# Adding the four channel tiles on GpSimd ahead of the mean matmul, and a bias copy issued from ScalarE

## What is computed

```python
h = rmsnorm(x, pre_norm_g[l])
u = h @ w_in[l]
q, k, v, g_att, c_val, c_glu, g_conv = jnp.split(u, split_pts, axis=-1)
a = chunk_attention(q, k, v, rel_bias[l]) * jax.nn.silu(g_att)
c = conformer_conv(c_val, c_glu, dw_w[l], dw_b[l], conv_ln_g[l], conv_ln_b[l],
                   w_pw[l], b_pw[l]) * jax.nn.silu(g_conv)
y = jnp.concatenate([a, c], axis=-1) @ w_out[l]
x = x + rmsnorm(y, post_norm_g[l])
```

## Time and profile before

| | us |
|---|---|
| median of 3 runs | 2664.9 |
| lowest and highest run | 2659.37, 2668.94 |
| span of the profiled execution | 2665.6 |
| PE busy | 2384.7 |
| DVE busy | 1711.2 |
| ACT busy | 962.0 |
| POOL busy | 292.4 |

### The profile page before, as it was taken

One profiled execution on the slowest core, in us unless ns is written; L12 is line 12 of the kernel. 1 busy time (PEld: TensorE's weight loads), 2 busy tenths in 40 slices (PEclk: granted clock), 3 DMA queues, 4 the chain that ended last, 5 costly groups with the idle time before them and its releaser, 6 DMA issues. The chain is left out here.

```text
span 2665.6 us, 45368 instructions
## 1 busy us (share of the span) xinstructions
PE 2384.7 (89%) x16468; PEld 2197.2 (82%) x16468; DVE 1711.2 (64%) x3174; ACT 962.0 (36%) x1803; POOL 292.4 (11%) x260
## 2 busy tenths in 40 slices
PE   5999999999997899999997889993898888889887
PEld 5999999999996889888986667782787778878886
DVE  5756656656557887888886534432666766676675
ACT  4111111111113221222121534432666666666664
POOL 0000000000000000000000000000322332232242
PEclk9999999999998999999998899995999999999998
DMA  5222222222224433332333342327466456646743
GB/s 176 100 96 73 92 87 75 95 82 86 99 71 153 163 115 138 135 128 105 131 123 112 105 119 90 126 75 207 113 172 160 119 151 163 162 120 177 179 119 119
DMA packets 207901, 327.46 MB, mean 123 GB/s; under 512 B 16625, under 2 KB 141561, under 8 KB 207768
## 3 DMA queue, kind: packets, MB, share of 16 engines
q1 hardware_dynamic: 206680, 324.69, 40.3%
q10 hardware_dynamic: 1088, 1.05, 0.2%
HBM read 198.24 MB, written 127.46 MB: 122 GB/s over the span
## 5 line engine op out<-in xcount | busy, mean ns | idle before, releaser
L261 PE MATMUL p_pb<-h_hT_hi,p_w_hi 128*128 128x256 f32 x3072 | 873.8, 284 | 39.4 <-DVE h_hT_lo L204 24.6
L263 PE MATMUL p_pb<-h_hT_hi,p_w_lo 128*128 128x256 f32 x3072 | 864.5, 281 | 0.0
L262 PE MATMUL p_pb<-h_hT_lo,p_w_hi 128*128 128x256 f32 x3072 | 864.4, 281 | 0.0
L261 PEld LDWEIGHTS p_pb<-h_hT_hi,p_w_hi 128*128 128x128 f32 x3072 | 581.7, 189 | 45.4 <-DVE p_st L455 22.6
L262 PEld LDWEIGHTS p_pb<-h_hT_lo,p_w_hi 128*128 128x128 f32 x3072 | 582.4, 190 | 0.7
L263 PEld LDWEIGHTS p_pb<-h_hT_hi,p_w_lo 128*128 128x128 f32 x3072 | 581.7, 189 | 0.0
L638 DVE SCALAR_TENSOR_TENSOR p_acc<-p_hgl,k_dwt,p_acc 128x512 f32<-128x512 f32 x544 | 368.3, 745 | 0.0
L423 DVE SCALAR_TENSOR_TENSOR p_acc<-p_hg,k_dwt,p_acc 128x256 f32<-128x256 f32 x832 | 337.3, 478 | 0.0
L1349 DVE CUSTOM_DVE_ANT_0 p_pr<-p_s,p_bias 128x640 f32<-128x640 f32 (+4 forms) x256 | 199.8, 781 | 207.0 <-PE p_s L1451 205.5
L1266 ACT ACTIVATE p_pr<-p_pr,p_nmax 128x640 f32<-128x640 f32 (+4 forms) x256 | 204.0, 797 | 189.2 <-DVE p_nmax L1349 187.1
L1451 PE MATMUL p_s<-p_ks,p_q_hi 128*128 128x384 f32 (+2 forms) x480 | 178.5, 376 | 103.0 <-DMA p_q_lo<-q_parts 61.7
(11 more groups left out here) (155 smaller groups left out, 3891.4 us busy)
## 6 DMA issues: line engine op xcount, KB each, us to landing
h_x<-in_x SPq DMA_DIRECT2D x32, 1024.0 KB, 6.3
q_parts<-p_st SPq DMA_DIRECT2D x64, 256.0 KB, 2.3
k_parts<-p_st SPq DMA_DIRECT2D x64, 256.0 KB, 2.4
v_parts<-p_vst SPq DMA_DIRECT2D x16, 1024.0 KB, 4.4
y_conv<-p_yst SPq DMA_DIRECT2D x64, 256.0 KB, 2.0
p_ks<-k_parts SPq DMA_DIRECT2D x32, 512.0 KB, 8.8
p_vs<-v_parts SPq DMA_DIRECT2D x16, 1024.0 KB, 11.5
p_y<-y_conv SPq DMA_DIRECT2D x16, 1024.0 KB, 6.3
```

The costliest lines, as they stand in the source:

```text
L261: nc.tensor.matmul(out, stat_hi(k), mov_hi(k), start=(k == 0), stop=False)
L262: nc.tensor.matmul(out, stat_hi(k), mov_lo(k), start=False, stop=False)
L263: mm = nc.tensor.matmul(out, stat_lo(k), mov_hi(k), start=False, stop=(k == tiles - 1))
```

## The change

POOL gets two additions per block: `pairs` (channel tiles 0 and 1 plus 2 and 3, 128x1024) and `total` (the two halves of `pairs`, 128x512). `mean` on PE becomes one matmul with `total`. PE now waits for `total_ok` where it waited for `acc_in`. POOL waits for `acc_in`, and before it overwrites `total` for `mean_ps` of the block before. The copy of `rev` moves from SP's stream (behind block 0's stores) to ACT's (behind block 0's copies of output units), with its wait for `rev_ok`; SP's block 0 goes into the loop.

```diff
+            def channels(i, first=False):
+                pool.wait_ge(acc_in, DMA * (i + 1))
+                nc.gpsimd.tensor_tensor(pairs[:, :, :], acc[:, 0:2, :], acc[:, 2:4, :], ALU.add).then_inc(pairs_ok, 1)
+                pool.wait_ge(pairs_ok, i + 1)
+                if not first:
+                    pool.wait_ge(mean_ps, i)
+                nc.gpsimd.tensor_tensor(total[:, :], pairs[:, 0, :], pairs[:, 1, :], ALU.add).then_inc(total_ok, 1)
...
-            body(0, 2)
-            sp.wait_ge(rev_ok, 2)
-            sp.dma_start(D["rev"], rev[:, None, :].broadcast_to([HEADS, P, 3 * P - 1])).then_inc(rev_out, DMA)
-            with sp.Fori(1, NBLK - 2) as i:
+            with sp.Fori(0, NBLK - 2) as i:
...
             body(0, False)
+            act.wait_ge(rev_ok, 2)
+            act.dma_start(D["rev"], rev[:, None, :].broadcast_to([HEADS, P, 3 * P - 1])).then_inc(rev_out, DMA)
             with act.Fori(1, NBLK - 1) as i:
...
             def mean(i, first=False):
-                pe.wait_ge(acc_in, DMA * (i + 1))
+                pe.wait_ge(total_ok, i + 1)
                 if not first:
                     pe.wait_ge(dev_ok, i)
-                for c in range(CT):
-                    mm = nc.tensor.matmul(mean_b[:, :], K["ones"][:, :], acc[:, c, :], start=(c == 0), stop=(c == CT - 1))
-                mm.then_inc(mean_ps, 1)
+                nc.tensor.matmul(mean_b[:, :], K["ones"][:, :], total[:, :], start=True, stop=True).then_inc(mean_ps, 1)
```

More of the change, by code:

```diff
@@ L730, in pass_3 @@
         sqs = T.sb("sqs", [P, 2, BLK])
+        pairs, total = T.sb("pairs", [P, 2, BLK]), T.sb("total", [P, BLK])
+        pairs_ok, total_ok = T.sem("pairs_ok"), T.sem("total_ok")
         var_s, rstd = T.sb("var", [P, 4]), T.sb("rstd", [P, 4])
@@ L789, in norm @@
                 nc.gpsimd.tensor_tensor(rstd[:, :], var_s[:, :], K["mhalf"][:, :], ALU.pow).then_inc(rstd_ok, 1)
-            with pool.Fori(0, NBLK) as i:
+            def channels(i, first=False):
[5 more added lines that the diff above has]
+                nc.gpsimd.tensor_tensor(total[:, :], pairs[:, 0, :], pairs[:, 1, :], ALU.add).then_inc(total_ok, 1)
+            channels(0, True)
+            norm(0)
+            with pool.Fori(1, NBLK) as i:
+                channels(i)
                 norm(i)
```

## The result

| | us |
|---|---|
| kernel before, median of 18 runs | 2668.35 (2659.37 to 2677.01) |
| changed kernel, median of 18 runs | 2656.43 (2650.78 to 2668.10) |
| ratio | 0.9962, 95% interval 0.9948 to 0.9975 |
| changed kernel, profiled execution | 2667.74, span 2666.0 |

By the ratio the change gains 0.38% (0.25 to 0.52), 10 us, where 25 were forecast; the two medians lie 11.9 us apart. The time lies outside the range of 2633 to 2655. In this comparison the kernel before took 3.4 us more than in the three runs that the forecast was set against; 0.9962 of those 2664.9 us is 2654.8, just inside the end of the range. That doesn't mend the forecast: less than half of the gain is there.

What follows compares the result with a forecast made beforehand. PE's own work and one stall in one block were taken to set pass 3's length. From 2665.6 us, 15.5 (mean) and 9.4 (copy) gave a span of 2640.7, a median of 2640 us; range 2633 to 2655.

Steps and rivals of the forecast that it cites:

- The mean on PE: Pass 3, blocks 2 to 7: six matmul records fewer save 2.6 us a block, 15.5 us in all.
- rival 1: Block 1 of pass 3: the stall stays, only the mean's gain is left, 12.9 to 16.5 us; chance 0.26.
- The additions on POOL: Pass 3 blocks: additions take 3.7 us, `total` is ready 10 us before PE asks for it; cost 0.
- The first two means: Start of pass 3, where PE isn't full: 0, with ends of 0.5 us won or 1.5 us lost.
- The copy of `rev`: Block 1 of pass 3: moving the copy to ACT's queue shortens PE's stall; gain 9.4 us.
- The first count: Stalled block: packets alternate, copy keeps its pace, PE stalls 2.8 us instead of 10.2; gain 9.4 us, chance 0.45.
- The second count: Stalled block: packets alternate and their times add up, PE stalls 9.1 us and drops its clock; gain 1 us.
- ACT and SP: Block 0 of pass 3: the copy's 1.20 us issue fits before ACT's square, cost 0; freed SP time gains 0.
- Rival 4: Block 0 of pass 3: ACT is held by the copy's issue, PE runs dry; 3.8 us slower, 2669; chance 0.03.

Runs made afterwards that it cites:

- second pair: The kernel before and the changed kernel, both unchanged, one more profiled execution each on one chip: 2664.9 and 2660.0 us.
- adds_only: The changed kernel with the copy of `rev` back in SP's stream: 2662.4 us beside 2672.7 for the kernel before, ratio 0.9961.
- copy_only: The kernel before with only the copy of `rev` moved to ACT: 2670.0 us, ratio 0.9990 (0.9971 to 1.0009).
- sixteen_timed: The changed kernel with `rev` on 16 partitions instead of 8, 64 repetitions from each: 2644.2 us beside 2667.6 for the kernel before, ratio 0.9910.
- wide: The changed kernel with `rev` on 128 partitions instead of 8, each written 8 times: 2649.9 us beside 2672.7 for the kernel before, ratio 0.9913.
- wide_sp: The kernel wide with its copy issued by SP, not ACT: 2644.3 us beside 2669.7 for the kernel before, ratio 0.9902.
- split: The changed kernel with the 8-partition copy issued from SP in eight pieces, one behind each block's stores: 2642.6 and 2646.8 us, ratios 0.9901 and 0.9923.

## Why the prediction was wrong

**The mean on PE: right.** 2.6 us a block was forecast. An ordinary block from `gc` to `gc` went from (241.1 - 50.7) / 5 = 38.1 us to (224.8 - 47.3) / 5 = 35.5. The timeline of PE, to be held against the earlier trace rows:

```profile
1577.58 1.02 PE L958 MATMUL p_mean<-p_total,k_ones 128*128 128x512 f32 x2
1578.03 0.79 PE L261 MATMUL p_pw<-p_s_hi,p_pw_hi 128*128 128x512 f32 x1
1578.66 0.39 PE L262 MATMUL p_pw<-p_s_lo,p_pw_hi 128*128 128x512 f32 x1
```

From the mean's start to the product's successor are 1.08 us; less 0.23 it is 0.43 for each of two records. But only five of the six blocks keep the saving. The sixth is the stalled one, where it is swallowed, as rival 1 had it.

**The additions on POOL: right on time, incomplete on cost.** POOL's timeline in a steady block:

```profile
1598.79 2.40 POOL L792 TENSOR_TENSOR p_pairs<-p_acc 128x1024 f32<-128x1024 f32 x1 [5.85 <-DMA p_acc<-conv]
1601.27 1.63 POOL L796 TENSOR_TENSOR p_total<-p_pairs 128x512 f32<-128x512 f32 x1
```

`total` is there at 1602.9, where 1603.5 was forecast; the next mean comes one block (35.5 us) after 1577.58, at 1613.1, so the cover is 10 us. No PE time is lost in any steady block. What the working didn't ask is what POOL's work does to DVE: 15.8 us more of busy time over 8 blocks, 2 us a block. DVE has room for that beside PE, everywhere but at the start.

**The first two means: a failed step, small.** Forecast 0, with ends of 0.5 us won and 1.5 us lost. The start takes 2.1 us longer (51.86 for 49.73; 2.3 in the second pair), beyond the lower end. The working asked when the mean is done. It was done about as worked out (2.04 us from 1487.17, which is 33.4 us after the pass's start; forecast 1485.4 - 1452.5 = 32.9). Two things came behind that. One it didn't have: DVE runs three two-input subtractions beside the additions. The other it named for the lower end and priced too low: PE, with less to do, gets its full clock about 10 us later. The first product comes 2.0 us later in the first pair and 0.5 in the second; how the loss divides between the two wasn't measured. The Trainium skill, page "SBUF — State Buffer", section "SBUF: two separate sides", says that VectorE with two inputs from SBUF and GpSimd share one pair of ports, and that one of them holds it for a whole instruction while the other is blocked. These rows agree in direction: DVE's three went from 3.49 to 6.00 us, and POOL's 128x512 took 2.12 us where pass 4 has 1.29; POOL's 128x1024 was not slower (2.35 us for 2.38).

**The copy of `rev`: the failed step that decides.** The first count took it that the copy's and SP's packets alternate on the shared engines from the issue of `gc` on, while the copy keeps its pace, so that `gc` and the first store are through at 1557.3, 19.5 us after the issue of `gc`. From that follow a stall of 2.8 us on PE and a gain of 9.4 us. What the runs showed in its place: for 14.3 us after its issue the shared half of `gc` isn't served at all, then the queues alternate, and the copy doesn't keep its pace (28 rows a us for 32). `gc` lands 23.2 us after its issue, `acc` 25.2 (25.6 before), the stall is 9.8 us, and the clock is at 0.50 behind it. In the sum, the gain of 9.4 us by the stall came out as 0.8: the stalled block costs 47.28 - 35.54 = 11.7 us more than an ordinary one, where before it cost 12.6 (11.8 in the second pair, and the gain there is nothing). By adds_only the 3.4 us by which that block is shorter divide otherwise: nothing for its mean, about 3 for the copy.

The second count (stall of 9.1 us, gain 1) came out nearly to the number, but by luck. It lets the packets alternate from the start at 0.34 us a pair. In the trace a pair takes 8 / 28 = 0.29 us on each of eight engines, and the time is lost ahead of the alternation, which no count had. Why it begins so late stays open.

Two things were wrong in choosing. The share of 1.13 from pass 4 was of transfers from and to 128 partitions, and was carried over to engines which one slow transfer keeps for 0.43 of the possible 0.50. And the row that said more was read for the queue alone: `acc`'s issue held for 4.42 us. It is held for 4.43 us when the copy isn't on SP's queue, so the copy's place in that queue can't have been the only reason.

The prediction leaned on the Trainium skill, page "DMA: Bandwidth & Descriptors", section "Queues, rings and completion order", for an alternation packet by packet. The section speaks of packets of several descriptors; the count took one row of 1.5 KB or 2 KB as a packet. The trace has both: 14 us without a switch, which doesn't fit row by row, and then 84 packets beside 84. The prediction's other rule, from the Trainium skill, page "DMA: Bandwidth & Descriptors", section "Issuing engines are not separate DMA queues", is that another issuer saves only the sequencer's time. The 15.5 us put down for it are nearer to the 10 us measured, and to the 13 to 14 us in pass 3, than the forecast's 24.9. The trace agrees with it but for some 2 us: counted from the issue of the copy, `gc` landed after 35.9 us, in adds_only after 37.6.

**ACT and SP: right.** The issue takes ACT 1.33 us, and the square still waits 2.65 us for DVE behind it, as forecast (2.7). Rival 4 didn't happen.

**Where the sum ends.** 15.5 + 9.4 - 0 = 24.9 became, in pass 3, 16.3 - 2.1 = 14.2 us (13.2 in the second pair): five means of 2.6, the stalled block shorter by 3.4 us, and 2.1 lost in the start. Rival 1 (the stall stays), with 12.9 to 16.5 us, is what happened in pass 3. The whole kernel shows 10 us, with an interval of 7 to 14. That pass 4 gave 3 us back is possible (868 to 874 us for 863 to 864.5) but two executions of each can't show it.

## What to carry to other kernels

In these runs the pace of a copy went with its source pattern, and a second queue took other transfers past it only late (after 14 us, and then row for row): read the share and the GB/s of the stretch in which it runs alone before you count on another queue, and widen the transfer over more partitions, or cut it so that it ends before the next one is due (here 12 us, where moving it brought about 3). Before shortening the work between two fixed events, ask what sets the later one: PE's saving in the block with the stall was swallowed because the stores came when the copy let them. And moving work from TensorE to GpSimd had a second price on VectorE, and went with a later full clock where TensorE had little to do; look for the place where VectorE is on the path or the clock has yet to rise, not at the blocks with room.

## What the runs showed of the hardware

- An SBUF-to-DRAM copy of 1532 KB in rows of 1532 bytes depends on the number of source partitions: from 8 it ran at 48 GB/s with a share of 0.43 (some 32 us, an estimate from its size and that rate), from 16 at 97 GB/s with 0.87 (landed after 18.8 us), from 128 it landed after 9.1 us. From 8 to 16 the share doubles, from 16 to 128 each engine gets faster. That a partition read over and over is the limit fits, but the repetitions, the number of partitions and the part of the 128 over which they spread changed together, and none was varied alone. The same 8 rows spread over all 128 partitions, for one, weren't tried.
- Beside a slow copy on ACT's queue, the part of SP's transfers on the same engines waited for 14.3 us after the issue (changed kernel), while the copy kept its 32 rows a us; then the two queues moved 84 packets each in 3 us, and the copy 28 rows a us. copy_only shows the same.
- SP's issue of `acc`, 0.41 us in other blocks, was held for 4.43 and 4.38 us with the slow copy on ACT's queue (after, copy_only), and for 4.42 and 5.53 us with it on SP's own (before, adds_only).
- In the start of pass 3 TensorE's granted clock first rose from 0.50 to 1.00 at 29 to 33 us after it had 5.3 to 6.0 us of matmuls in the second mean or while it ran them, and at 41 to 44 us where the second mean was 2.0 us with a gap of 2.1 us behind it (five and nine traces).
- Three VectorE subtractions of 128x1024 with both inputs in SBUF took 3.49 us alone, and 5.09 to 6.16 us beside GpSimd's additions (nine traces, from sixteen_timed to wide).
- Pass 4's length differed between kernels that differ only in pass 3. The eight traces with the copy on ACT's queue have 862.9 to 874.2 us (mean 868.0), the six with it on SP's 857.7 to 865.6 (mean 862.4); without the two of split these are 863.0 to 865.6. What of this is chance and what belongs to the queue wasn't tested. It is as large as what separates the best versions here, so which of wide_sp, split and sixteen is the fastest stays open; all are 20 us or more ahead of the kernel before, and by their ratios some 10 to 16 us ahead of the changed one.
